# Weight slabs loaded in transfers of 1 MB (two ring tiles of four slabs) in place of 512 KB (four ring tiles of two slabs)

## What is computed

```
p = rms_norm(x) @ w_in                                  # 2048 x 5008
h = x + concat(rwkv7(p), sparse_attention(p)) @ w_mix_out
h = h + cross_attention(h, mem; w_q_cross, w_kv_cross, w_o_cross)
h = h + relu(rms_norm(h) @ w_up)**2 @ w_down             # 2048 x 8192 and 8192 x 2048
x = rms_norm(h)
g = merged_attention(rms_norm(concat(meta, x)) @ w_in_2) @ w_out_2 + ...
q = rms_norm(g) @ peer_w_query                          # 16384 experts, then gathers
out = g + sum over 128 chosen experts of gelu(u . x) * v
```

## Time and profile before

| | |
|---|---|
| Three timed runs | 3894.45, 3895.01, 3912.82 us (median 3895.01) |
| The profiled execution, its own time | 3889.03 us |
| Span of the profiled execution | 3887.1 us |
| Busy: TensorE, POOL, DVE, ACT | 70%, 65%, 43%, 29% of the span |
| Mean granted TensorE clock | 0.83 |
| SP's queue (all weight loads) | 161600 packets, 313 MB, 26.9% of 16 engines' span |

### The profile page before, as it was taken

The page is one execution under the profiler, slowest core; times in us unless marked ns, Lnnn a source line. Parts: engine busy times, 40 slices in busy tenths (PEclk is TensorE's granted clock), DMA queues, the critical chain, the costliest instruction groups (busy, mean ns, idle before and its releaser), DMA issues.

```text
span 3887.1 us, 40212 instructions
## 1 busy us (share of the span) xinstructions
PE 2722.8 (70%) x14616; PEld 2139.0 (55%) x14616; DVE 1670.1 (43%) x2168; ACT 1146.2 (29%) x2149; POOL 2528.9 (65%) x1831
## 2 busy tenths in 40 slices
PE   6982658979799999997999888850006883002887
PEld 5861438967699789986999556850002331001333
DVE  3000264461323002202000452299999747997444
ACT  5440222234544444444444565520000000000000
POOL 6871650048489899897888405768884547887442
PEclk9995768989999999999999858985557886555888
DMA  5551320005356566564666203469998999999997
GB/s 162 180 182 56 96 87 1 1 1 164 114 163 187 173 184 184 170 188 138 174 174 174 87 1 125 147 243 416 427 427 365 427 427 427 427 427 427 427 427 325
DMA packets 253493, 867.78 MB, mean 223 GB/s; under 512 B 33090, under 2 KB 35154, under 8 KB 186386
## 3 DMA queue, kind: packets, MB, share of 16 engines
q0 software_dynamic: 74496, 539.59, 33.0%
q1 hardware_dynamic: 161600, 313.43, 26.9%
q10 hardware_dynamic: 17248, 12.81, 1.1%
HBM read 860.24 MB, written 2.10 MB: 222 GB/s over the span
## 4 chain that ended last, share of the span: by engine, by line
PE 52%; DVE 17%; POOL 13%; issue 8%; DMA 7%; ACT 2%; ACTq 1%; DVEq 0%; POOLq 0%
PE acc L1589 19%; PE acc L1584 18%; DVE zone L1504 8%; DMA zone<-in_peer_v,zone 7%; PE acc L2013 6%; POOL zone L635 5%; PE acc L1676 5%; POOL w_lo L521 4%; POOL lasting L635 4%; DVE x_lo L1108 1%; PE acc L1832 1%; ACTq L647 1%; DVE zone L1251 0%; PE acc L1819 0%; PE acc L1688 0%
## 5 line engine op out<-in xcount | busy, mean ns | idle before, releaser
L521 POOL TENSOR_TENSOR w_lo<-lasting,w_hi 128x512 fp32r<-128x512 f32 (+1 forms) x1184 | 1572.9, 1345 | 597.1 <-ACT w_hi L675 564.3
L2013 PE MATMUL acc<-zone,lasting 128*128 128x512 f32 x1024 | 517.5, 670 | 781.9 <-DMA zone<-in_peer_v,zone 781.9
L675 ACT ACTIVATE w_hi<-lasting 128x512 fp32r<-128x512 f32 (+1 forms) x1184 | 743.7, 633 | 1058.7 <-PE acc L1584 499.6
L2013 PEld LDWEIGHTS acc<-zone,lasting 128*128 128x128 f32 x1024 | 218.1, 216 | 1080.7 <-issue 1080.7
L1530 DVE SCALAR_TENSOR_TENSOR lasting<-lasting,zone 128x2048 f32<-128x2048 f32 x128 | 301.0, 2352 | 240.4 <-DMA lasting<-in_peer_v,zone 232.0
L1589 PE MATMUL acc<-x_hi,w_hi 128*128 128x256 f32 (+1 forms) x2112 | 343.9, 285 | 16.6 <-DVE x_lo L1108 14.5
L1589 PE MATMUL acc<-x_lo,w_hi 128*128 128x256 f32 (+1 forms) x2112 | 340.3, 283 | 0.0
L1589 PE MATMUL acc<-x_hi,w_lo 128*128 128x256 f32 (+1 forms) x2112 | 340.0, 283 | 0.0
L1584 PE MATMUL acc<-w_hi,x_hi 128*128 128x512 f32 (+1 forms) x736 | 242.6, 412 | 135.8 <-POOL w_lo L521 123.8
L635 POOL DMA_INDIRECT zone<-in_peer_v,zone x128 | 181.8, 1420 | 218.1 <-PE acc L2013 186.1
L1504 DVE CUSTOM_DVE_ANT_0 zone<-lasting,zone 128x2048 f32<-128x2048 f32 x128 | 293.4, 2293 | 28.2 <-DMA lasting<-in_peer_u,zone 15.2
(11 more groups left out here) (370 smaller groups left out, 3485.2 us busy)
## 6 DMA issues: line engine op xcount, KB each, us to landing
lasting<-in_w_in SPq DMA_DIRECT2D x200, 512.0 KB, 3.6
lasting<-in_w_up SPq DMA_DIRECT2D x128, 512.0 KB, 3.8
lasting<-in_w_down SPq DMA_DIRECT2D x128, 512.0 KB, 4.6
lasting<-in_w_mix_out SPq DMA_DIRECT2D x32, 512.0 KB, 3.9
lasting<-in_w_out SPq DMA_DIRECT2D x32, 512.0 KB, 4.4
lasting<-in_peer_w_query SPq DMA_DIRECT2D x32, 512.0 KB, 3.9
lasting<-in_w_kv_cross SPq DMA_DIRECT2D x16, 512.0 KB, 3.7
lasting<-in_w_q_cross SPq DMA_DIRECT2D x8, 512.0 KB, 3.7
```

The lines of the kernel that those rows point to most:

```text
L521: pool.tensor_tensor(w_lo[:, k, 0:width], ring[:, slot, s % SLOT_SLABS, 0:width], w_hi[:, k, 0:width].bitcast(FP32), ALU.subtract).then_in ...
L675: act.activation(w_hi[:, s % PARTS, 0:width], ring[:, slot, s % SLOT_SLABS, 0:width], ACT.Copy).then_inc(hi_ready, 1)
L2013: last = pe.matmul(bank(4 * t + c), diag[:, n // 2, j], rows_buf[4 * n + j][:, c * CHUNK:(c + 1) * CHUNK], start=i == 0 and n == 1 and j = ...
```

## The change

The two numbers that shape the ring trade places: four tiles of two slabs become two tiles of four slabs. The ring keeps its 8 slabs (2 MB) at the same place. All else is derived from the two numbers.

```
@@ -47,8 +47,8 @@
 WI0 = KI0 + I_HEAD
 
 CHUNK = 512
-SLOTS = 4
-SLOT_SLABS = 2
+SLOTS = 2
+SLOT_SLABS = 4
 PARTS = 4
 AHEAD = 3
 NEG = -1.0e30
```

## The result

| | before | 1 MB loads |
|---|---|---|
| Median | 3895.97 us (15 runs) | 3922.0 us (15 runs) |
| Profiled execution: its time, its span | 3889.03, 3887.1 us | 3917.54, 3915.8 us |
| Mean granted TensorE clock | 0.830 | 0.829 |

The ratio is **1.0061, interval 1.0041 to 1.0081**: slower by 0.6%, about 24 us (the medians are 26 us apart). I had forecast 49 us, 1.3%. The direction held, and so did the mechanism in the up products; the size was half, because the cost forecast for the down products and `out2` did not come.

A forecast was written before the change was run, and what follows sets the result against it. TensorE was taken to set the pace, POOL close behind. Terms 1 + 22 + 6 + 22 + 4 + 4 - 10 = + 49 us on 3889.0 gave 3938, with 6 us for the median 3944 us; range 3915 to 3985 (0.62).

The forecast's parts named there:

- What bounds it, and the 5.1 us: Product stages: TensorE sets the pace, POOL nearly full; a load may take 5.1 us, excess paid once per 8 slabs.
- one of my signs of being wrong: Anywhere in the products: the forecast is wrong if ACT waits for weights but TensorE doesn't, because POOL catches up.
- L of 1 MB: Landing time of a 1 MB weight load: the 512 KB landing plus 1.4 us everywhere, plus 1.8 us in down1.
- + 1.8 in `down1`: In down1: 1 MB lands after 4.7 + 1.8 = 6.5 us, 1.4 over the limit, 16 loops: 22 us.
- the slow kind: 512 KB loads of w_down and w_out landing after 4.7 to 4.8 us, against 3.9 in other chunks.
- The up products: In up0 and up1: late tiles plus rests slowed by DVE's eviction cost 1.4 us a chunk, 16 chunks, 22 us.
- The shifted copy: Around that copy: ring filled with 8 slabs instead of 10, up to two slabs left over at its end: 4 us.
- The lead of 10 us: Rests are ready some 2 us early; 2.1 us eaten first in each of five products that are over: - 10 us.
- Hidden anyway: Rival: 1 MB lands within about 4.6 us, so losses sum to 5 to 15 us, about 3903 us; chance 0.17.
- worse: Rival: each 512 KB adds 2.3 us everywhere, another 95 us over some 106 loops, about 4040 us; chance 0.16.
- faster: Rival: fewer loads beside the shifted copy let it end sooner, 10 us, if loads also fit; about 3885 us; chance 0.05.
- The loop formula: Time round one ring tile: landing, first rounding, four rests, handing on, L + 6.0 us, against eight slabs of TensorE.

The follow-up runs named there:

- One_at_a_time: Kernel before (512 KB loads), but in down0 and down1 SP issues a load only when the one before has landed; 4011.43 us, single execution.
- quiet_1mb: Changed kernel (1 MB loads) with DVE's eviction of the up products cut to one pass, so another output; 3894.43 us, ratio 0.9998.
- pairs_late: Kernel before (512 KB loads), but loads released two at a time, when the changed kernel releases one 1 MB load; 3901.78 us, ratio 1.0007.
- late_1mb: Changed kernel with every 1 MB load released one slab later, SP waiting for one rest more; 4308.25 us, ratio 1.105, four runs.

## Why the prediction was wrong in size

- **What bounds it, and the 5.1 us.** Right. ACT waits for nearly every load in the up and down products, but only in the up products is TensorE late by it. `w_down` at 5.1 us lies at the limit and costs nothing (- 0.1 and - 0.2 us in `down0`, `down1`). There one of my signs of being wrong came true: ACT waits and TensorE doesn't.
- **L of 1 MB.** "+ 1.4 everywhere" was right for `w_in` and `w_up` (5.0 and 5.2). `mix` and `out2` have 5.1 and `query` 5.0, where the quick 512 KB loads of such matrices take 3.7 to 3.9: + 1.1 to + 1.4.
- **The step that failed: "+ 1.8 in `down1`", on top of 4.7 us.** I took the slow kind as a property of these loads that 1 MB inherits, and added to it. 22 us in `down1`, 4 of the 6 in `down0` and 4 in `out2` rest on it, and the other 2 in `down0` on 5.3 us where 5.1 was measured: 32 of the 59 us before the deduction. They measured - 0.1 (`down0`), - 0.2 (`down1`) and + 0.7 us (`out2`), with these loads at 5.1 us (median), and 0.7 us more ahead of `down0` and of `down1`. One_at_a_time shows that the 0.9 us go away where no load is issued before the last one has landed, and the change itself brings nearly that about. The better step was at hand: a load that is released half as often seldom meets its successor. (Also, by my own limit + 1.4 in `down1` would have given 16 us and not 14.)
- **The up products.** 22 us, less their share of the lead (two products, 4 us): 18; measured 15.5. That the 22 came so near is partly luck: I took 1.4 us a chunk by judgement, between 1.7 and 0.2, and the timeline above has 1.3 (23.98 against 22.7). The reason, late tiles and rests slowed by DVE together, is shown by quiet_1mb.
- **The shifted copy.** 4 us; measured 2.5, and pairs_late shows it to go with the release, as I had put it.
- **The lead of 10 us.** Taken off in five products; three of them were not over and had nothing to take it from. With the right L the sum is 1 + 22 + 4 - 4 = 23 us, where 24 were measured, and 20.7 by the stages; it has neither the small terms (1.3 us in `cross_o`, 1.4 in `sb_q`) nor the 3.2 us that the gathers gave back.
- **The rivals.** "Hidden anyway" needed landings of at most 4.6 us and "worse" some 0.9 more than the 5.0 to 5.2 that came; "faster" needed an earlier end of the shifted copy, and DVE waits 283.4 us for it where it waited 283.6. What counts in this ring is how soon the first slab is there: 5.2 us in the changed kernel, 4.0 in pairs_late. The rule of the Trainium skill ("DMA: Bandwidth & Descriptors", section "Bandwidth") to batch to 1 MiB gave no gain here. By the fit in the same page's section "Anatomy of one DMA — SWDGE (gpsimd) path", made for DMAs issued from GpSimd, a 1 MB load would take 4.4 us, an estimate; these loads are issued by SP, and this trace has 5.0 to 5.2. The Trainium skill's "Perfetto Trace Analysis", section "DMA Optimizations", says that splitting may let some parts start sooner, for engines that are generally idle; here they were 0.5 to 0.6 busy, and pairs_late agrees in that its first half lands sooner.

The loop formula itself has a limit that I learnt only from late_1mb: it is one of two conditions. A release must also not depend on a rest of the tile that is still on its way.

## What to carry to other kernels

In a ring of fixed memory the size of a transfer is part of a loop: landing time, first use, all uses of the tile, release. Work out that loop against the pace of the bound engine, with the slowest uses and not the mean ones, for each stage by itself. Here it cost nothing up to the limit (5.1 us in the down products) and 1.3 us a chunk just over it, and with two tiles one slab less of distance made them wait for each other. And a landing time read where transfers overlap need not hold for a size at which they don't.

## What the runs showed of the hardware

- In the matrices `w_in` and `w_up`, 256, 512 and 1024 KB land after 2.8 to 2.9, 3.6 to 3.8 and 5.0 to 5.3 us (medians), so the second 512 KB took 1.4 us and halving 512 KB saved only 0.7 to 0.9.
- 512 KB loads of a matrix 2048 columns wide, issued every 2.8 us, landed some 0.9 us later in some chunks than in others (in `w_down` 4.5 to 4.9 against 3.7 to 4.0 us, medians of chunks); issued only after the last one had landed, they took 3.65 to 3.84 us in all eight chunks of `w_down` (one execution).
- While the copy from SBUF to SBUF of 127 partitions runs, ACT got 1 MB after 20.5 us (394.22 - 373.68) where it had got 512 KB every 10.7: nearly the same rate at both sizes.

```profile
373.68 2.19 ACT L675 ACTIVATE w_hi<-lasting 128x512 fp32r<-128x512 f32 x4 [22.55 <-DMA lasting<-in_w_in]
394.22 2.19 ACT L675 ACTIVATE w_hi<-lasting 128x512 fp32r<-128x512 f32 x4 [18.35 <-DMA lasting<-in_w_in]
```

- The recurrent part took 386 to 412 us in the traces of these kernels, at a mean granted clock of 0.84 and 0.79 in the two looked at above. It is most of what makes executions differ: the kernel with 256 KB loads has spans of 3892.4 and 3886.6 us in its two traces, and without this part 3499.5 and 3499.9.
